# LRU gates per head side by side in the matmul array, and the next row's copy and first convolution term on VectorE

## What is computed

```
xc, lru_conv_new = causal_dwconv(u_lru, lru_conv_prev, w_lconv, b_lconv)     # width 4
h, lru_h_new = rg_lru(xc, lru_h_prev, w_a, b_a, w_i, b_i, lam)
br_lru = (h * jax.nn.gelu(y_lru)) @ w_br_lru
...
r = jax.nn.sigmoid(block_diag(x, w_a, b_a))          # 16 blocks of 64 x 64
i = jax.nn.sigmoid(block_diag(x, w_i, b_i))
log_a = -LRU_C * r * jax.nn.softplus(-lam)
a = jnp.exp(log_a)
bterm = jnp.sqrt(-jnp.expm1(2.0 * log_a)) * i * x
h = scan over positions of  h = a * h + bterm
```

## Time and profile before

| what | before |
|---|---|
| median of 3 runs | 1825.24 us (1821.39 to 1827.02) |
| the profiled execution's own time | 1824.54 us |
| its span, first to last instruction | 1822.8 us |
| TensorE busy | 1801.9 us (99%) |
| VectorE, ScalarE, GpSimd busy | 836.8, 560.5, 510.2 us |
| LRU stage | about 514 us to 722 us of the span |

### The profile page before, as it was taken

The page is one execution under the profiler, slowest core; times in us unless marked ns, Lnnn a source line. Parts: engine busy times, 40 slices in busy tenths (PEclk is TensorE's granted clock), DMA queues, the critical chain, the costliest instruction groups (busy, mean ns, idle before and its releaser), DMA issues.

```text
span 1822.8 us, 29780 instructions
## 1 busy us (share of the span) xinstructions
PE 1801.9 (99%) x11252; PEld 1753.1 (96%) x11252; DVE 836.8 (46%) x1580; ACT 560.5 (31%) x1108; POOL 510.2 (28%) x283
## 2 busy tenths in 40 slices
PE   8899999999999999999999999999999999999999
PEld 8898888899999999999999999999999999999999
DVE  7746757711246666112464555411555511555511
ACT  5425544400156766112133322200222300333300
POOL 2511111123323232332222333222233333332222
PEclk9989989999999999999999999999999999999999
DMA  4101000111111111111311111111111111111113
GB/s 150 35 30 35 32 12 26 34 38 46 46 50 40 40 49 38 47 46 46 142 46 35 46 46 46 46 46 46 46 44 38 45 46 46 46 46 46 46 46 120
DMA packets 28514, 89.21 MB, mean 49 GB/s; under 512 B 3472, under 2 KB 8496, under 8 KB 28464
## 3 DMA queue, kind: packets, MB, share of 16 engines
q1 hardware_dynamic: 25200, 82.52, 14.0%
q10 hardware_dynamic: 3264, 5.98, 1.0%
HBM read 83.74 MB, written 4.75 MB: 49 GB/s over the span
## 4 chain that ended last, share of the span: by engine, by line
PE 95%; DVE 2%; ACT 1%; POOL 1%; issue 0%; DMA 0%; SPq 0%; ACTq 0%; DVEq 0%; POOLq 0%
PE banks L403 85%; PE banks L523 2%; PE banks L538 2%; PE banks L512 1%; PE banks L479 1%; PE banks L489 1%; POOL w_hi L382 1%; PE banks L673 1%; PE banks L672 1%; DMA resid<-xT 0%; DVE x_lo L1137 0%; ACT prB L865 0%; PE banks L471 0%; DMA w_raw<-W 0%; DVE sqsum L1178 0%
## 5 line engine op out<-in xcount | busy, mean ns | idle before, releaser
L403 PE MATMUL banks<-x_hi,w_hi 128*128 128x354 f32 (+1 forms) x1776 | 588.4, 331 | 12.9 <-POOL w_lo L384 8.1
L403 PE MATMUL banks<-x_lo,w_hi 128*128 128x354 f32 (+1 forms) x1776 | 578.8, 326 | 0.0
L403 PE MATMUL banks<-x_hi,w_lo 128*128 128x354 f32 (+1 forms) x1776 | 575.2, 324 | 0.0
L382 POOL TENSOR_SCALAR w_hi<-w_raw 128x1024 fp32r<-128x1024 f32 x139 | 171.1, 1231 | 1281.0 <-DMA w_raw<-W 1281.0
L403 PE MATMUL banks<-h_hi,w_lo 128*128 128x354 f32 (+1 forms) x1152 | 373.9, 325 | 0.0
L403 PE MATMUL banks<-h_lo,w_hi 128*128 128x354 f32 (+1 forms) x1152 | 373.6, 324 | 0.0
L403 PE MATMUL banks<-h_hi,w_hi 128*128 128x354 f32 (+1 forms) x1152 | 373.3, 324 | 0.0
L403 PEld LDWEIGHTS banks<-x_hi,w_hi 128*128 128x128 f32 x1776 | 336.8, 190 | 17.5 <-POOL w_lo L384 8.4
L384 POOL TENSOR_TENSOR w_lo<-w_raw,w_hi 128x1024 fp32r<-128x1024 f32 x139 | 338.5, 2436 | 11.6
L403 PEld LDWEIGHTS banks<-x_lo,w_hi 128*128 128x128 f32 x1776 | 336.8, 190 | 2.9
L403 PEld LDWEIGHTS banks<-x_hi,w_lo 128*128 128x128 f32 x1776 | 336.2, 189 | 0.0
(11 more groups left out here) (205 smaller groups left out, 1767.0 us busy)
## 6 DMA issues: line engine op xcount, KB each, us to landing
w_raw<-W SPq DMA_DIRECT2D x140, 512.0 KB, 3.4
sqsum<-xT ACTq DMA_DIRECT2D x2, 2120.0 KB, 12.2
o_yT<-resid SPq DMA_DIRECT2D x8, 530.0 KB, 5.0
resid<-xT SPq DMA_DIRECT2D x4, 708.0 KB, 8.2
resid<-xT SPq DMA_DIRECT2D x2, 704.0 KB, 11.3
wabs<-wab ACTq DMA_DIRECT2D x8, 128.0 KB, 2.0
mat<-mats SPq DMA_DIRECT2D x1, 192.0 KB, 10.2
vec<-vecs SPq DMA_DIRECT2D x1, 143.0 KB, 2.2
```

Source lines behind the costliest of these rows:

```text
L382: nc.gpsimd.tensor_scalar(w_hi[s][:, :], w_raw[s][:, :], 1.0, 0.0, ALU.mult, ALU.add).then_inc(w_hi_done, 1)
L403: last = nc.tensor.matmul(out[:, 0:cn], w[s][:, k * P:(k + 1) * P], x[:, k, cc:cc + cn], start=(k == 0 and j == 0), stop=(k == KT - 1 and ...
```

## The change

The two gate matmuls of `lru_gates` no longer hold a block diagonal each. One matmul reads partitions 0 to 63 (the first block of 64 channels) and writes bank 6, the other reads partitions 64 to 127 and writes bank 7; each has a 64 x 128 weight with the block's a matrix and its i matrix side by side. For the first block the a gate comes out on partitions 0 to 63 and the i gate on 64 to 127, for the second block the other way round. ScalarE then needs four activations with 64 partitions in place of two with 128 to move a chunk's gates into FA and FI. The weight tile `wabs` has half its size. The copies of U out of PSUM and the convolution's first term move from ScalarE to VectorE: the copies to the head of the turn, the first term ahead of each chunk's three taps.

```diff
@@ matmul engine
 def lru_gates(j, n):
     pe.wait_ge(r_xc, j * 3 + (n + 1))
     pe.wait_ge(r_tanh, j * 3 + (START + n))
-    nc.tensor.matmul(bank[6][:, 0:cn], wabs[:, 0, :], XC[n][:, 0:cn], start=True, stop=True)
-    nc.tensor.matmul(bank[7][:, 0:cn], wabs[:, 1, :], XC[n][:, 0:cn], start=True, stop=True).then_inc(r_ps, 1)
+    for e in range(2):
+        of = slice(HD * e, HD * e + HD)
+        last = nc.tensor.matmul(bank[6 + e][:, 0:cn], wabs[of, :], XC[n][of, 0:cn], start=True, stop=True)
+    last.then_inc(r_ps, 1)
...
-    tile(0, j, PAIR_R + 1, x_hi, x_lo, x_act, j * 3 + (X_ACT["R"] + 3))
+    tile(0, j, PAIR_R + 1, x_hi, x_lo, x_dve, j * 3 + (X_DVE["R"] + 3))
@@ ScalarE
 def lru_decay(j, n):
     wait(r_ps, j * 3 + (n + 1))
-    A(FA[:, ck], bank[6][:, 0:cn], ACT.Tanh, bias=halfb[:, cols(j + 2 * KT, 1)], scale=0.5)
-    A(FI[:, ck], bank[7][:, 0:cn], ACT.Tanh, bias=halfb[:, cols(j + 3 * KT, 1)], scale=0.5).then_inc(r_tanh, 1)
+    for e in range(2):
+        here, there = slice(HD * e, HD * e + HD), slice(HD - HD * e, P - HD * e)
+        A(FA[here, ck], bank[6 + e][here, 0:cn], ACT.Tanh, bias=halfb[here, cols(j + 2 * KT, 1)], scale=0.5)
+        last = A(FI[here, ck], bank[6 + e][there, 0:cn], ACT.Tanh, bias=halfb[there, cols(j + 3 * KT, 1)], scale=0.5)
+    last.then_inc(r_tanh, 1)
...
 with act.Fori(0, KT - 1) as j:
-    wait(r_xc, j * 3 + 2)
-    lru_u(j + 1, 0)
-    wait(r_xc, j * 3 + 3)
-    lru_u(j + 1, 1)
-    lru_u(j + 1, 2)
     wait(r_lo, j * 3 + START)
     for n in range(3):
         lru_decay(j, n)
-        if n < 2:
-            wait(r_in, j * 3 + (n + 1))
-            wait(r_fix, j + 2)
-            lru_x0(j + 1, n)
     load_wab(j + 1)
     lru_root(j)
-    lru_x0(j + 1, 2)
     lru_gelu(j + 1)
     lru_hi(j)
@@ VectorE
 def lru_history(j):
-    dve.wait_ge(x_act, j * 3 + (X_ACT["R"] + 3))
+    for n, (c0, cn) in enumerate(CHUNKS):
+        dve.wait_ge(x_done, j * 3 + (3 * PAIR_R + n + 1))
+        D.tensor_copy(U[:, LRU_HIST + c0:LRU_HIST + c0 + cn], bank[n][:, 0:cn]).then_inc(x_dve, 1)
+    dve.wait_ge(x_dve, j * 3 + (X_DVE["R"] + 3))
...
 def lru_conv(j, n):
-    dve.wait_ge(r_x0, j * 3 + (n + 1))
+    link(D.tensor_scalar(XC[n][:, 0:cn], U[:, 3 + c0:3 + c0 + cn], VD("conv_w", j * 4 + 3), VD("conv_b", j), ALU.mult, ALU.add))
     for tap in (2, 1, 0):
```

More of the change, by code:

```diff
@@ L55 @@
 X_ACT = dict(R=out_before(PAIR_B))
-X_ACT["G0"] = X_ACT["R"] + 3 * KT
+X_ACT["G0"] = X_ACT["R"]
 X_ACT["F"] = X_ACT["G0"] + 3
@@ L59 @@
 Y_ACT["G0"] = Y_ACT["R"] + 3 * KT
-X_DVE = dict(B=3, G0=3 + 3 * KT // 2)
+X_DVE = dict(B=3, R=3 + 3 * KT // 2, G0=3 + 3 * KT // 2 + 3 * KT)
 X_DVE["O"] = X_DVE["G0"] + 3 * (KT - 1)
@@ L182, in build @@
         XC = [sb(f"XC{i}", [P, 354]) for i in range(3)]
-        wabs = sb("wabs", [P, 2, P])
+        wabs = sb("wabs", [P, P])
         at = [tr]
@@ L264, in build @@
                                       "p_copied", "out", "hi", "lo"))
-        r_fix, r_x0, r_xc, r_ps, r_tanh, r_in, r_sqa, r_om, r_root, r_h, r_z, r_hi, r_lo = (
-            sem(f"lru_{x}") for x in ("history", "x0", "xc", "psum", "tanh", "inputs", "a_squared", "one_minus_a2", "root", "h",
+        r_xc, r_ps, r_tanh, r_in, r_sqa, r_om, r_root, r_h, r_z, r_hi, r_lo = (
+            sem(f"lru_{x}") for x in ("xc", "psum", "tanh", "inputs", "a_squared", "one_minus_a2", "root", "h",
                                       "z", "hi", "lo"))
@@ L651, in gated @@
                 xa, ya, xd = X_ACT[stage], Y_ACT[stage], X_DVE[stage]
-                tile(0, 0, p0, x_hi, x_lo, x_act, xa)
+                tile(0, 0, p0, x_hi, x_lo, x_dve, xd)
                 if between is not None:
@@ L671, in lru_gates @@
                 pe.wait_ge(r_tanh, j * 3 + (START + n))
-                nc.tensor.matmul(bank[6][:, 0:cn], wabs[:, 0, :], XC[n][:, 0:cn], start=True, stop=True)
-                nc.tensor.matmul(bank[7][:, 0:cn], wabs[:, 1, :], XC[n][:, 0:cn], start=True, stop=True).then_inc(r_ps, 1)
-            tile(0, 0, PAIR_R, x_hi, x_lo, x_dve, X_DVE["G0"])
+                for e in range(2):
+                    of = slice(HD * e, HD * e + HD)
+                    last = nc.tensor.matmul(bank[6 + e][:, 0:cn], wabs[of, :], XC[n][of, 0:cn], start=True, stop=True)
+                last.then_inc(r_ps, 1)
+            tile(0, 0, PAIR_R, x_hi, x_lo, x_dve, X_DVE["R"])
             tile(1, 0, PAIR_R, x_hi, x_lo, y_dve, Y_DVE["G0"])
             with pe.Fori(0, KT - 1) as j:
-                tile(0, j, PAIR_R + 1, x_hi, x_lo, x_act, j * 3 + (X_ACT["R"] + 3))
+                tile(0, j, PAIR_R + 1, x_hi, x_lo, x_dve, j * 3 + (X_DVE["R"] + 3))
                 pe.wait_ge(s_wab, j * 16 + 16)
@@ L980, in load_wab @@
             def load_wab(j):
[L981 to L994, removed]
+                src = wab[j] if isinstance(j, int) else wab[bass.ds(j, 1)].rearrange("a p n -> (a p) n")
+                act.dma_start(wabs[:, :], src).then_inc(s_wab, 16)
             def lru_decay(j, n):
@@ L1352, in lru_history @@
             def lru_history(j):
-                dve.wait_ge(x_act, j * 3 + (X_ACT["R"] + 3))
+                if not isinstance(j, int):
+                    dve.wait_ge(r_xc, j * 3)
+                for n, (c0, cn) in enumerate(CHUNKS):
+                    dve.wait_ge(x_done, j * 3 + (3 * PAIR_R + n + 1))
+                    D.tensor_copy(U[:, LRU_HIST + c0:LRU_HIST + c0 + cn], bank[n][:, 0:cn]).then_inc(x_dve, 1)
+                dve.wait_ge(x_dve, j * 3 + (X_DVE["R"] + 3))
                 for r, c0 in enumerate((SEQ, T)):
-                    D.tensor_copy(st_lconv[:, cols(j, 1), r, :].rearrange("p a n -> p (a n)"), U[:, c0:c0 + LRU_HIST])
-                D.tensor_copy(U[:, SMP:SMP + LRU_HIST], VD("conv0", j * LRU_HIST, LRU_HIST)).then_inc(r_fix, 1)
+                    ins = D.tensor_copy(st_lconv[:, cols(j, 1), r, :].rearrange("p a n -> p (a n)"), U[:, c0:c0 + LRU_HIST])
+                link(ins)
+                link(D.tensor_copy(U[:, SMP:SMP + LRU_HIST], VD("conv0", j * LRU_HIST, LRU_HIST)))
             def lru_conv(j, n):
                 c0, cn = CHUNKS[n]
-                dve.wait_ge(r_x0, j * 3 + (n + 1))
+                if not isinstance(j, int):
+                    dve.wait_ge(r_in, j * 3 + (n - 2))
+                link(D.tensor_scalar(XC[n][:, 0:cn], U[:, 3 + c0:3 + c0 + cn], VD("conv_w", j * 4 + 3), VD("conv_b", j), ALU.mult, ALU.add))
                 for tap in (2, 1, 0):
@@ L1403, in _ @@
             with dve.Fori(0, KT - 1) as j:
-                ch.enter(j, 2 * 3 + 1)
+                ch.enter(j, 3 * 3 + 1 + 2)
                 lru_history(j + 1)
@@ L1572 @@
     xT[:, :SEQ], xT[:, SMP:] = x["x_prompt"][0].T, x["x_sample"][0].T
-    wab = np.zeros((KT, P, 2, P), f32)
+    wab = np.zeros((KT, P, P), f32)
     for m, name in enumerate(("w_lru_a", "w_lru_i")):
@@ L1577 @@
             for e in range(2):
-                wab[j, HD * e:HD * e + HD, m, HD * e:HD * e + HD] = x[name][0, 2 * j + e]
+                at = HD * (m ^ e)
+                wab[j, HD * e:HD * e + HD, at:at + HD] = x[name][0, 2 * j + e]
     sink = x["attn_sink"][0]
@@ L1583 @@
                  conv_w=x["w_lru_conv"][0].reshape(4, KT, P).transpose(2, 1, 0).reshape(P, -1), conv_b=_cols(x["b_lru_conv"][0]),
-                 b_a=_cols(x["b_lru_a"][0]), b_i=_cols(x["b_lru_i"][0]), lam=_cols(x["lru_lambda"][0]),
+                 b_a=_cols(x["b_lru_a"][0]), b_i=np.roll(_cols(x["b_lru_i"][0]), HD, axis=0), lam=_cols(x["lru_lambda"][0]),
                  g_mix=_cols(x["g_mix"][0]), g_ffn=_cols(x["g_ffn"][0]),
```

## The result

| | before | after |
|---|---|---|
| median of 4 runs each, side by side | 1823.32 us (1819.89 to 1827.02) | 1846.16 us (1845.84 to 1848.26) |
| span of the profiled execution | 1822.8 us | 1846.5 us |

The changed kernel is slower: ratio 1.0125, interval 1.0108 to 1.0142. That is 22.8 us by the medians and 23.7 us by the two profiled spans; 12.3 were forecast. The direction and the place are right, the size is nearly twice the forecast, and the median lies just above the upper end of the range.

What follows compares the result with a forecast made beforehand. The matmul engine bound the kernel, the ScalarE and VectorE loop 0.41 us behind; a loop turn of 28.42 us then sets the pace: 10.4 us over seven turns plus 2.7 in the tail give 1837.5 us, range 1820 to 1846.

Steps and rivals of the forecast that it cites:

- The matmul engine: Gates' matmuls: a call falls from 1.19 to 0.99 us, the engine's own turn from 26.85 to 26.25 us.
- both passages: Matmul engine's changes of shape around a gates' call: 0.19 us to enter, 0.20 to leave.
- The moves: Copies and first terms to VectorE: copies cost nothing; ScalarE loses 1.18 us of first terms per turn.
- The first term of chunk 2: On VectorE between the scan's products and `lru_lo`: +0.45 us per turn, range 0.40 to 0.55.
- The added tanh: ScalarE's two more tanh per chunk, 0.45 us each: +0.90 per chunk, +2.70 us per turn.
- its bounds: ScalarE's tanh: if other start partitions prevent overlap, three distances become 0.55 us, 0.3 more per chunk.
- The first turn: First turn of the LRU stage: still follows the gates, so costs +1.0 us in place of 1.57.
- The tail: After the seven turns: three decays, no first term to lose, +2.7 us.
- behind it nothing is changed: After `lru_lo` of row 7, where matmuls resume: the rest unchanged, so the span grows by the same 13.1 us.
- I expect it at full speed: Matmul engine's clock in the turns: stays full though the engine idles 2.2 us in 28.
- The loop is longer still: Rival, chance 0.18: activations on different partitions don't overlap, +6.3 us in turns, 0.9 in the tail; 1845 up to 1848.
- The matmul engine as the bound: Rival, chance 0.17: the ScalarE and VectorE loop stays under 26.25 us per turn, giving 1820.5 us.

Runs made afterwards that it cites:

- e7: Changed kernel with two tanh of 128 partitions per chunk in place of four, so partitions 64 to 127 compute something else: 1818.80 us, ratio 0.9972.
- e8: Changed kernel with `lru_lo` ahead of the third chunk's convolution on VectorE: 1833.84 us, ratio 1.0065 to the kernel before.
- e1: Kernel before with only the copies of U and the convolution's first term moved to VectorE: 1824.57 us beside 1825.48, ratio 1.000.
- e4: Changed kernel with GpSimd's split of one second weight tile held back until `lru_lo` of row 7 is done: 1844.72 us, ratio 1.0106 to before.
- e3: Kernel before with each tanh of 128 partitions cut into two of 64, matmuls unchanged: 1847.49 us beside 1825.48, ratio 1.0134.
- e2: Changed kernel with the copies of U and the first terms back on ScalarE: 1849.21 us beside 1825.48 for the kernel before, ratio 1.0138.
- e9: Changed kernel with `lru_lo` ahead of the third chunk's convolution and GpSimd's split held back in the tail: 1832.72 us, ratio 1.0044 to before.

## Why the prediction was off by ten microseconds

**The matmul engine, right.** Its own turn was forecast at 26.25 us and is 26.2 in e7 and in the first turns of e8. Passes run in two pairs, with both passages priced about right. That the packed matmuls would gain nothing, because the loop becomes the bound, held.

**The moves, right.** The copies were forecast at nothing, and e1 shows nothing. The first term of chunk 2 was to cost 0.45 us and takes 0.50; product to `lru_lo` in a turn went from 9.83 to 10.63 us, +0.80, where first term and contention together were to give 0.75. The splits now meet VectorE earlier in its chain, as the prediction said: in the turn from 573.23 the scan takes 4.37 us in place of 2.29, and the three products are back at 1.40.

**The added tanh, the step that failed.** "So I take the full 0.45 for each of the two more: +0.90 per chunk, +2.70 per turn." Measured: +1.24 per chunk and 3.7 per turn. The full cost of half a tile was right; that the overlap of the earlier trace rows would be kept was not. The prediction had it among its bounds, 0.3 more per chunk, and in the rival with 0.18. Part of it came back. From the second chunk's square to the third chunk's first tanh it was 552.73 - 550.86 = 1.87 us and is 583.18 - 582.77 = 0.41; from the first chunk's square to the second's tanh it was 548.25 - 547.20 = 1.05 and is 578.92 - 578.52 = 0.40. That is 2.11 us less where 1.86 were counted, and 0.1 more went inside the first chunk. So the turn grew by 2.26 us, not 1.59: 29.09 against 28.42. The first turn cost 1.06 (forecast 1.0) by the starts of row 1's first tanh, 1.41 if it is counted from the first gates, which stand 0.35 us earlier. Up to row 7's first tanh that makes 14.5 for 10.4.

**The tail, right in one half.** Its three decays cost 3.7 us for 2.7, the same 1.0 us as in a turn. What wasn't priced at all is the other half: "behind it nothing is changed". GpSimd's splits, which began behind the products before, now meet them, +3.0 us (e4 takes them off); and the idle matmul engine comes back at half its clock, +2.2. The prediction had looked at both mechanisms, at the contention for the turns and at the clock for idle time spread over a turn, and not at one place where they come together. Its "I expect it at full speed" failed in the turns too, where the clock fell twice; there the matmul engine had time to spare, and it cost nothing. Terms: 4.1 + 1.0 + 3.0 + 2.2 = 10.3 of the 10.6 us that separate 13.1 from 23.7.

**The rivals.** "The loop is longer still", with its 1845 to 1848, is the one that happened, through the mechanism that it names. That its sum also fits is in part chance: it took +6.3 us for the turns and 0.9 for the tail, and found were 4.1 and 1.0 over the forecast; the other 5.2 us are the tail's contention and clock, which it didn't have. The matmul engine as the bound needs tanh under 0.1 us more; e7 is the kernel in which that is so.

## What to carry to other kernels

In these traces an activation costs by its columns and not by its partitions. Before cutting one by partitions to suit a matmul, count each piece at its full duration, without the overlap, and look which chain that engine stands in: here 0.21 us saved per call on the engine that was 99% busy cost 1.24 on one that was 31% busy. Find out first how near the second chain is: one wait of ScalarE for the matmuls, 0.41 us in 27, was the whole distance. And where a chain moves against a second engine, ask again what lies over each of its instructions at the new time, above all in the tail, where a wait is paid in full and can cost clock too, a wait of 2.0 us in one profile and not in another. Where two kernels differ by a few microseconds, compare their profiles from a common mark inside the stage.

## What the hardware showed unexpectedly

- A tanh of 64 partitions and 354 columns takes 0.55 us, as one of 128 does; two tanh follow each other after 0.45 to 0.46 on the same partitions, and after 0.55 to 0.57 if input or output partitions change (e3, after). The first tanh behind a first term of 128 partitions lost the overlap in e3 (0.71) and kept it in e2 (0.59), though both begin at partition 0; the last read of PSUM before it began at partition 64 in e3 and at 0 in e2.
- The two matmuls on different rows of the array need no pairing in the program: four passes of a call fit in some 0.9 us against 1.19, and change of shape included they save 0.21 us per call (e7).
- Three VectorE products of 1.39 us took 4.37 us under GpSimd's splits of 1.25 and 2.49 us (after) and 1.39 with these held back (e4).
- In a wait of 5.0 us the granted clock fell to 0.50 before the matmuls resumed and stayed there until 4.9 us after the matmuls had resumed (after). After waits of 2.0 us the clock stayed full in e4 and e3 and fell 0.6 us after the matmuls had resumed in e9. Waits of 1.9 to 2.0 us inside a turn were followed by a fall twice (after).
